# Panel steps laid anew around the waits of a hybrid mixer, and the last quarter of two output panels taken for one token tile first

## The reference

```
proj = h @ w_in                       # 2048 -> q 1024, k 128, v 128, dn q/k/v 3x1024, z 1024, a 8, b 8
sq, sk = rope(q), rope(k)
attn_out = sliding_window_attention(sq, sk, v, sinks)          # 16 query heads, 2 key/value heads, window 128
dn q, k, v = silu(causal_conv(dn_qkv));  q, k l2-normalised     # 8 heads of 128
o = gated_delta_rule(q, k, v, g, beta)                         # S <- exp(g)(I - beta k k^T) S + beta k v^T ; o = S^T q
o = o * rsqrt(mean(o*o)) * dn_norm_w * silu(z)
mix = concat([attn_out, o]) @ w_out                            # 2048 -> 2048
x = layer_norm(ALPHA * x + mix)
```

## Time and profile before

| | |
|---|---|
| median of 3 runs | 2086.16 us (2084.18 to 2086.24) |
| the profiled execution | 2083.27 us |
| its span | 2081.5 us |
| PE busy | 1951.6 us, 94% of the span, 10877 matmul records |
| DVE busy | 652.9 us, 31% |
| ACT busy | 342.5 us, 16% |
| DMA | 539.00 MB, 259 GB/s over the span, 420 GB/s and more in the experts |
| mean granted clock of TensorE | 0.98 of full speed |

### The profile page before, as it was taken

The page is one execution under the profiler, slowest core; times in us unless marked ns, Lnnn a source line. Parts: engine busy times, 40 slices in busy tenths (PEclk is TensorE's granted clock), DMA queues, the critical chain, the costliest instruction groups (busy, mean ns, idle before and its releaser), DMA issues.

```text
span 2081.5 us, 26748 instructions
## 1 busy us (share of the span) xinstructions
PE 1951.6 (94%) x10877; PEld 1125.7 (54%) x10877; DVE 652.9 (31%) x1287; ACT 342.5 (16%) x622; POOL 16.8 (1%) x106
## 2 busy tenths in 40 slices
PE   8999999999799999999799999999998999999995
PEld 4688866664544344344347888566545444434442
DVE  1235545531611111111332536545324111111015
ACT  0104220110311111111211132201104111101112
POOL 3000000000000000000000000000000000000000
PEclk9999999999899999999999999999998999999998
DMA  7434342205599999999945433422246999999995
GB/s 243 147 126 142 104 146 95 81 14 210 202 409 422 422 422 422 422 422 422 386 131 166 136 122 123 141 72 71 109 145 267 421 422 422 422 422 422 422 422 240
DMA packets 128831, 539.00 MB, mean 259 GB/s; under 512 B 15856, under 2 KB 20464, under 8 KB 78320
## 3 DMA queue, kind: packets, MB, share of 16 engines
q1 hardware_dynamic: 128752, 537.86, 66.2%
HBM read 535.73 MB, written 2.10 MB: 258 GB/s over the span
## 4 chain that ended last, share of the span: by engine, by line
PE 64%; DMA 30%; DVE 4%; issue 1%; SPq 1%; ACT 1%; DVEq 0%
PE bank L718 20%; PE bank L707 16%; DMA x_t<-in_w_up_dram 15%; DMA x_t<-in_w_down_dram 15%; PE bank L1130 7%; PE bank L1167 5%; PE bank L957 3%; PE bank L742 3%; PE bank L1086 2%; PE bank L653 1%; PE bank L829 1%; PE bank L844 1%; PE bank L1098 0%; SPq L580 0%; PE bank L928 0%
## 5 line engine op out<-in xcount | busy, mean ns | idle before, releaser
L707 PE MATMUL bank<-x_t,ring 128*128 128x256 f32 x1536 | 346.8, 384 | 0.0
L707 PEld LDWEIGHTS bank<-x_t,ring 128*128 128x128 f32 x1536 | 291.5, 192 | 50.2 <-issue 11.9
L718 PE MATMUL bank<-ring,x_t 128*128 128x512 f32 (+1 forms) x640 | 257.5, 554 | 1.9 <-DMA ring<-in_w_in_dram 1.9
L1130 PE MATMUL bank<-ring,prob_t 128*64 128x512 f32 x768 | 173.5, 594 | 31.7 <-DMA ring<-in_w_up_dram 31.7
L1940 DVE TENSOR_TENSOR region_a<-bank,region_a 128x512 f32<-128x512 f32 x16 | 11.1, 692 | 578.1 <-PE bank L1130 578.1
L718 PE MATMUL bank<-ring,mix_acc 128*128 128x512 f32 x384 | 181.3, 613 | 1.4 <-ACT mix_acc L1353 1.4
L718 PEld LDWEIGHTS bank<-ring,x_t 128*128 128x128 f32 x640 | 118.6, 190 | 112.5 <-issue 105.2
L1130 PEld LDWEIGHTS bank<-ring,prob_t 128*64 128x64 f32 x768 | 57.9, 137 | 143.9 <-issue 143.9
L1086 PEld LDWEIGHTS bank<-prob_t,x_nat 128*128 128x128 f32 x1024 | 118.6, 196 | 14.4 <-issue 11.4
L1086 PE MATMUL bank<-prob_t,x_nat 128*128 128x128 f32 x1024 | 121.6, 281 | 2.8 <-DVE prob_t L1874 2.8
L1130 PE MATMUL bank<-ring,region_a 128*64 128x512 f32 x512 | 113.4, 595 | 0.0
(11 more groups left out here) (364 smaller groups left out, 1941.5 us busy)
## 6 DMA issues: line engine op xcount, KB each, us to landing
ring<-in_w_gate_dram SPq DMA_DIRECT2D x96, 1024.0 KB, 21.5
ring<-in_w_in_dram SPq DMA_DIRECT2D x80, 1024.0 KB, 5.0
ring<-in_w_up_dram SPq DMA_DIRECT2D x64, 1024.0 KB, 19.1
region_b<-in_w_down_dram SPq DMA_DIRECT2D x48, 1024.0 KB, 22.0
ring<-in_w_out_dram SPq DMA_DIRECT2D x32, 1024.0 KB, 5.1
region_b<-in_w_gate_dram SPq DMA_DIRECT2D x32, 1024.0 KB, 21.1
x_t<-in_w_up_dram SPq DMA_DIRECT2D x32, 1024.0 KB, 23.5
ring<-in_w_down_dram SPq DMA_DIRECT2D x32, 1024.0 KB, 20.6
```

Source lines behind the costliest of these rows:

```text
L707: m = pe.matmul(b[c // 2][:, (c % 2) * T:(c % 2 + 1) * T], w[:, kk, c * P:(c + 1) * P], xT[:, k, :], start=(k == 0 and c % 2 == 0), stop=( ...
L718: m = pe.matmul(b[t][:, 0:width], lhs[:, k, t * P:(t + 1) * P], w[:, kk, 0:width], start=(k == 0), stop=(k == KC - 1))
L1130: m = pe.matmul(bank[2 + w][rows, :], xg_half[k // 8][:, k % 8 * P + rows.start:k % 8 * P + rows.stop], exp_slot[(n + e) % EXP_SLOTS][:, k ...
```

## The change

In `k_step`, the wait for heads 4 to 7 now depends on the tile: a step for tile 0 alone waits for the third turned block, one with tile 1 for the fourth. The signal that frees a ring slot goes to the first tile of the step, whichever that is. Two of the four chunks of panel 3 go ahead of query group 3. In the delta rule the counts of `meanwhile` are laid anew, and the last quarters of panels 11 and 12 are split: seven of the eight tile steps for tile 0 come between the transposes of tile 0 and tile 1 of the second half, the eighth between tile 1's steps of panel 11 and of panel 12, so that the order of `proj_done` stays.

```
-                    if i in (11, 12) and k in (8, 12) and tiles[0] == 0:
-
-                        pe.wait_ge(to_read.sem, to_read.at(l, k // 2 - 2))
+                    if i in (11, 12) and k == 8 and tiles[0] == 0:
+                        pe.wait_ge(to_read.sem, to_read.at(l, 2))
+                    if i in (11, 12) and k == 12:
+
+                        pe.wait_ge(to_read.sem, to_read.at(l, 3 + tiles[-1]))
...
-                            if t == 0:
+                            if t == tiles[0]:
                                 settle(m)
...
                     if g == 3:
+                        panel(3, 0, 2)
                         pe.wait_ge(tq_read.sem, tq_read.at(l, 1))
...
-                panel(3, 0, 4)
+                panel(3, 2, 4)
...
+                last_quarters = [(i, k) for i in (11, 12) for k in range(12, KC)]
+
                 def turn_out(half):
                     for t in range(NT):
                         n = 2 * half + t
                         if n == 1:
-                            meanwhile(4)
+                            meanwhile(5)
+                        if n == 3:
+                            meanwhile(len(left))
+                            for i, k in last_quarters[:-1]:
+                                k_step(i, k, (0,))
                         pe.wait_ge(dn_out.sem, dn_out.at(l, n + 1))
...
                         if t == 0 and half == 1:
+                            meanwhile(1)
                             pe.wait_ge(o_ready.sem, o_ready.at(l, 1))
                             pe.wait_ge(to_read.sem, to_read.at(l, 2))
...
-                        meanwhile(5 if half == 0 else 4)
+                        meanwhile(5 - half)
                         pe.wait_ge(pair_read.sem, pair_read.at(l, n + 1))
...
-                        meanwhile(4 if half == 0 else 3)
+                        meanwhile(3 + t - half)
...
                     for h in range(HALF):
                         pe.matmul(bank[6][:, h * P:(h + 1) * P], q_h[:, h, P:T], state(h), start=True, stop=True)
-                    meanwhile(2)
                     pe.wait_ge(v1_ready.sem, v1_ready.at(l, half + 1))
...
                     if half == 1:
-                        meanwhile(len(left))
+                        meanwhile(2)
                         pe.wait_ge(o_ready.sem, o_ready.at(l, 2))
                     turn_out(half)
-                panel(11, 12)
-                panel(12, 12)
+                for i, k in last_quarters:
+                    if (i, k) == (12, 12):
+                        k_step(12, KC - 1, (0,))
+                    k_step(i, k, (1,))
                 panel(13)
```

## The result

The changed kernel takes 2060.11 us in the median of four runs (2059.35 to 2061.47), the kernel before 2086.2 us in the same comparison (2084.18 to 2086.77). The ratio is 0.9878, with a 95% interval of 0.9866 to 0.9890: 26.1 us faster. The profiled execution took 2059.35 us with a span of 2057.5 us, 24.0 us less than the profiled one before; the prediction had 2057.8 for the profiled time and 2060.7 for the median.

The account below looks back on a forecast made before the run. PE, busy 94% of the span, bounds the kernel; only idle and lower-clock time can be won. Gains 10.9 + 3.4 + 11.2 = 25.5 us off 2083.27 give 2057.8 us, median 2060.7 us, range 2055 to 2067.

Parts of the forecast that it names:

- The sum: Whole kernel: gains of 10.9, 3.4 and 11.2 us make 25.5 us; 2057.8 us profiled, plus 2.9 us for the median.
- Panel 3: Query group 3: two chunks ahead cover its wait for ACT's copy and avoid the lower clock; 10.9 us over both layers.
- Half 0: Delta rule's first half: line 1031 starts 1.69 us earlier, shorter waits behind it; 1.7 us per layer, 3.4 us in all.
- Half 1: Second half and last quarters: the dn_out wait and lower clock go; 5.74 + 5.48 = 11.2 us.
- longer experts: Sign against the forecast: experts taking longer than before, though they were expected to move as one block.
- Two prices of one wait: Long PE waits: PE stands still, then runs at half speed, 1.2 instead of 2.4 GHz.
- The 6 us to spare: Half 1, tile 1's transposes: with 9.5 us of tile steps ahead, their input is done by 6 us.
- Nothing can be put there, as all else is for tile 1: Behind tile 1's transposes in half 1: the 1.01 us wait for ACT's copy must stay uncovered.
- (a): Rival at the wait ahead of (11, 12), tile 1: clock falls, costing 5.4 us, 2066.1 us; chance 8%.
- (b): Rival at the softmax between scores and probs_ready: panel 3's 10.9 us are given back, 2071.6 us; chance 5%.
- (c): Rival at panel 13, chunk 4, both layers: piece (13, 1) lands late, slower than before, 2091 us; chance 2%.
- (d): Rival at the new places: steps don't cover as counted, each place keeps half its wait, 2073 us; chance 3%.

Follow-up runs that it names:

- panel 3's part alone: Kernel before with only two of panel 3's four chunks moved ahead of query group 3: 2076.73 us, ratio 0.9955.
- one chunk ahead: Changed kernel with one chunk of panel 3 ahead of query group 3 instead of two: 2062.21 us, ratio 0.9887.
- the run with only four ahead: Changed kernel with only four tile steps of chunks 8 to 11 ahead of tile 1's transposes, all sixteen last-quarter steps behind: 2058.89 us, ratio 0.9876.

## Why the prediction was right

**The sum.** 25.5 us were forecast against the profiled time, 25.4 us are found in the mixers' stretches. Panel 3: 10.9 forecast, 5.74 + 5.09 = 10.8 found. Half 0: 3.4 forecast, 3.3 found; line 938 starts 8.40 us after line 1037, 8.36 were worked out. Half 1: 11.2 forecast, 11.3 found. The profiled execution got only 23.9 us of that, since the part from the second layer's first scatter took 1.0 us more, the second router 0.4 us and the start 0.2 us. The next profile of the same kernel has 457.1 us in that last part, as before, and 1.5 us more across the first layer's router. The prediction had named longer experts as a sign that it was wrong. The sign came up in the first profile and not in the second, and over the twelve profiles this part takes 457.1 to 458.2 us, so it is scatter. The wait for a piece in `conv_sq`, 0.2 us before and 1.2 us after, doesn't explain it: runs without that wait take up to 458.2 us there.

That the median came out 0.6 us from the forecast is in part luck: the profiled execution was 1.6 us above its sum, while the 2.9 us added for the difference between it and the median were 0.8 us in the changed kernel.

**Two prices of one wait.** That the idle time and the half-speed stretch behind it go together is shown by panel 3's part alone and by one chunk ahead: the first frees both, the second leaves 1.3 and 1.6 us idle and no loss of clock.

**Half 0.** The forecast gain came, and the two steps ahead of line 1031 did cover nothing. But the earlier start of line 1031, by which the prediction counts the gain, doesn't pay by itself: with these steps put back, half 0 takes 10.07 us for eight steps, where the kernel before took 10.05 us for six. What pays are the steps at the two waits.

**Where the reasoning fell short.** The range and the total were right, but one step took the seven tile steps of the last quarters for the cover of tile 1's transposes: "PE has eleven tile steps (9.5 us) ahead of tile 1's transposes, so that they find their input done by 6 us". Four did, and the run with only four ahead is no slower. The 6 us to spare, worked out in the prediction itself, should have said that the steps were in the wrong place. Nor does the prediction see that the first of these seven need ACT's copy of tile 0, which the four steps ahead of them cover; without those PE waits 1.60 us. And "Nothing can be put there, as all else is for tile 1" was wrong: of the seven steps for tile 0 any that stand ahead can stand behind, and two of them there took 0.95 us off each layer.

**The rivals.** (a) The clock did not fall at the remaining wait in either of the changed kernel's two profiles, nor behind waits of 1.08 and 1.39 us in the run with one chunk ahead. But it did fall once behind waits of 1.08 and 0.78 us, in panel 3's part alone, for 1.6 us. The rule that I cited from the Trainium skill ("TensorE: Matmul & The Clock Gate", section "A second HAM failure mode: psum-queue depth-cycling"), that brief idling between groups can make the clock swing, there in a bf16 kernel, so has one case here. Half 0's pair of short waits stands in two traces with two layers each, the kernel before and panel 3's part alone, and the clock fell in one of the four. Behind the last quarters' single wait it fell in none of the twelve stretches of the six traces in which the stretch has that wait and no other (22.77 or 22.78 us each). So 8% were not too much. (b) No gain was given back at the softmax: the stretch from the key transposes to the first spread is 216.19 to 216.20 us in every trace. (c) The late piece: the margin was 4.8 us, 5 were worked out, and holding it back by 8.7 us brought the wait, but nothing near what would make the kernel slower than before. (d) The covers held: no new waits in the list, and the stretches with the inverse, behind which panel 10's last step stands, take 54.72 to 54.73 and 53.01 us as before.

## What to carry to other kernels

Before moving work to cover a wait, write down for each wait when its input comes and how much work already stands ahead of it; what is more than that should stand ahead of the next wait. Here eleven steps stood where four were enough, none stood where two were missing, and moving two was worth the idle time they covered, 0.95 us in each layer. A wait of 3.1 to 3.6 us cost PE one and a half to nearly two times its length here (5.76 us for 3.08, 5.10 for 3.38, 5.5 for 3.57), because the granted clock fell to 0.50 behind it, so partial cover that brought it to 1.3 and 1.6 us won most of the price. And edits that cover for each other can't be priced by leaving out one at a time: undone singly they cost nothing and 3.5 us, together 11.3 us, all by the stretches.

## What the runs showed of the hardware that I had not expected

The clock's answer to short waits isn't the same each time: with the same waits of 1.08 and 0.78 us and the same instructions it stayed at 1.00 in three stretches and fell to 0.50 in one. And the scatter between profiles lies in a few places: the mixers' stretches repeat to 0.02 us over twelve profiles wherever the instructions are the same and the clock stays up, while the start of the program took from 86.1 to 89.2 us to the query transposes, the router between mixer and experts from 57.9 to 61.0 us, and the last part, from the second layer's first scatter on, from 457.1 to 458.2 us. That the spread of 1 to 4 us between executions of one kernel is made in the same places is likely but not shown, since each run left the trace of one execution. A difference of 1 us in a mixer can be read from one profile, where the medians of four runs don't show it.
